# Softmax scaling on GpSimd and half the turned-probability copies on VectorE in the first block's attention

## What is computed

```python
def block_attention(q, k, v):            # q blocks of 128 rows
    s = jnp.einsum('bqhgd,bkhd->bhgqk', qi, k) * scale
    p = jax.nn.softmax(s, -1)
    return jnp.einsum('bhgqk,bkhd->bqhgd', p, v)
...
att_l = block_attention(q_l, [k_l; k_c], [v_l; v_c])
att_c = block_attention(q_c, k_c, v_c)   # layer 0 only
```

## Time and profile before

| what | us |
|---|---|
| median of three runs | 1950.0 |
| the three runs | 1945.93, 1950.0, 1954.12 |
| profiled execution, from its first to its last instruction | 1946.4 |
| attention of layer 0, from the first exponential to the last low part | 216.4 to 275.1 |
| attention of layer 1, the same | 849.5 to 887.3 |

### The profile page before, as it was taken

The page is one execution under the profiler, slowest core; times in us unless marked ns, Lnnn a source line. Parts: engine busy times, 40 slices in busy tenths (PEclk is TensorE's granted clock), DMA queues, the critical chain, the costliest instruction groups (busy, mean ns, idle before and its releaser), DMA issues.

```text
span 1946.4 us, 34448 instructions
## 1 busy us (share of the span) xinstructions
PE 1835.5 (94%) x15010; PEld 1624.3 (83%) x15010; DVE 1155.6 (59%) x1715; ACT 769.5 (40%) x1073; POOL 296.1 (15%) x264
## 2 busy tenths in 40 slices
PE   7999788999999988988999999989999999999998
PEld 5777556778888868857999999989988888899997
DVE  4644665654353347666665586555768778677654
ACT  4433563221122224355334443333455544344342
POOL 0011001999080010100000100003001111000000
PEclk9999999999999999899999999999999999999999
DMA  8245112666353222203555555544431112255551
GB/s 350 94 172 200 56 44 87 197 208 198 121 191 112 88 76 71 82 22 109 181 187 178 194 203 176 193 152 150 142 141 45 46 45 67 88 176 189 178 192 69
DMA packets 40759, 266.24 MB, mean 137 GB/s; under 512 B 4512, under 2 KB 4640, under 8 KB 13344
## 3 DMA queue, kind: packets, MB, share of 16 engines
q1 hardware_dynamic: 35712, 244.10, 36.2%
q0 software_dynamic: 4608, 16.78, 2.8%
q10 hardware_dynamic: 288, 3.15, 0.4%
HBM read 262.96 MB, written 1.05 MB: 136 GB/s over the span
## 4 chain that ended last, share of the span: by engine, by line
PE 77%; DVE 11%; ACT 5%; POOL 4%; issue 2%; DMA 1%; SPq 0%; DVEq 0%; ACTq 0%; POOLq 0%
PE ps L641 19%; PE ps L643 19%; PE ps L642 19%; DVE W L621 3%; PE ps L1666 2%; POOL work L1126 2%; DMA ring<-w_ada_dram 1%; PE ps L1028 1%; ACT W L612 1%; POOL work L1127 1%; PE ps L1453 1%; DVE work L821 1%; PE ps L2407 1%; PE ps L2425 1%; PE ps L647 1%
## 5 line engine op out<-in xcount | busy, mean ns | idle before, releaser
L621 DVE TENSOR_TENSOR W<-ring,W 128x2048 fp32r<-128x2048 f32 (+2 forms) x194 | 441.8, 2279 | 238.7 <-ACT W L612 238.4
L612 ACT ACTIVATE W<-ring 128x2048 fp32r<-128x2048 f32 (+2 forms) x194 | 359.0, 1853 | 114.0 <-PE ps L643 104.9
L641 PE MATMUL ps<-h_lat,W 128*128 128x256 f32 x1056 | 301.7, 286 | 5.9 <-DVE h_lat L813 4.0
L642 PE MATMUL ps<-h_lat,W 128*128 128x256 f32 x1056 | 300.6, 285 | 0.0
L643 PE MATMUL ps<-h_lat,W 128*128 128x256 f32 x1056 | 300.5, 285 | 0.0
L641 PEld LDWEIGHTS ps<-h_lat,W 128*128 128x128 f32 x1056 | 204.3, 193 | 7.1 <-issue 4.6
L642 PEld LDWEIGHTS ps<-h_lat,W 128*128 128x128 f32 x1056 | 204.2, 193 | 0.3 <-issue 0.2
L643 PEld LDWEIGHTS ps<-h_lat,W 128*128 128x128 f32 x1056 | 204.2, 193 | 0.0
L754 POOL TENSOR_TENSOR work<-work 128x256 f32<-128x256 f32 (+1 forms) x42 | 41.0, 976 | 951.8 <-ACT work L736 764.8
L1009 DVE TENSOR_TENSOR work<-work,ps 128x256 f32<-128x256 f32 (+1 forms) x88 | 43.0, 488 | 181.7 <-ACT work L984 181.6
L643 PE MATMUL ps<-hidden_lat,W 128*128 128x256 f32 x528 | 149.7, 284 | 0.0
(11 more groups left out here) (405 smaller groups left out, 4285.4 us busy)
## 6 DMA issues: line engine op xcount, KB each, us to landing
ring<-w_up_dram SPq DMA_DIRECT2D x88, 1024.0 KB, 4.9
ring<-w_down_dram SPq DMA_DIRECT2D x43, 1024.0 KB, 4.9
ring<-w_ada_dram SPq DMA_DIRECT2D x32, 1024.0 KB, 6.6
work<-w_ada_dram POOLq DMA_DIRECT2D x32, 512.0 KB, 4.2
ring<-w_rkv_dram SPq DMA_DIRECT2D x13, 1024.0 KB, 4.9
ring<-w_fm_dram SPq DMA_DIRECT2D x10, 1024.0 KB, 4.9
ring<-w_out_dram SPq DMA_DIRECT2D x8, 1024.0 KB, 4.9
ring<-w_gates_dram SPq DMA_DIRECT2D x16, 512.0 KB, 3.7
```

The lines of the kernel that those rows point to most:

```text
L612: act.activation(slots[SLOT[s]][:, 0, 0:cols], ring[:, u % RING, 0:cols], ACT.Copy).then_inc(w_high, 1)
L621: dve.tensor_tensor(slots[SLOT[s]][:, 1, 0:cols], ring[:, u % RING, 0:cols], slots[SLOT[s]][:, 0, 0:cols], ALU.subtract).then_inc(w_low, 1)
L641: pe.matmul(o, slots[SLOT[s]][:, 0, at:at + cols], high, start=first, stop=False)
L642: pe.matmul(o, slots[SLOT[s]][:, 0, at:at + cols], low, start=False, stop=False)
```

## The change

In both layers of the first block's attention, GpSimd multiplies the `probs` tile by the reciprocal of its sum in place of VectorE, in a loop over the units, `pool_attention`, that is put between `pool_mlstm` and `pool_sums`. VectorE keeps the reciprocal. The copy of the turned probabilities stays with ScalarE for even units and goes to VectorE for odd ones. VectorE issues the copy of unit i-3 in its step i (even i from 4 on), behind maximum and negative of unit i and ahead of the reciprocal of unit i-1. Three semaphores come in: `at_recip` (VectorE to GpSimd), `at_even` and `at_odd` (the copies). TensorE now waits for `at_even` and `at_odd` where it waited for `at_pt`, at the same places of its order. The second block's attention only counts `at_pt` from another start.

```diff
@@ pe_attention
-                    pe.wait_ge(at_pt, base + 2 * p + 2)
+                    pe.wait_ge(at_even, base // 2 + p + 1)
+                    pe.wait_ge(at_odd, base // 2 + p + 1)
...
-                            pe.wait_ge(at_pt, base + x - 1)
+                            pe.wait_ge(at_odd if x % 2 else at_even, base // 2 + x // 2)
@@ act_attention
-                if 2 <= i < n + 2:
+                if 2 <= i < n + 2 and i % 2 == 0:
                     x = i - 2
...
-                    act.activation(probsT[x % 4][:, 0:nk], ps[:, 6 + x % 2, 0:nk], ACT.Copy).then_inc(at_pt, 1)
+                    act.activation(probsT[x % 4][:, 0:nk], ps[:, 6, 0:nk], ACT.Copy).then_inc(at_even, 1)
@@ dve_attention
+                if 4 <= i < n + 4 and i % 2 == 0:
+                    x = i - 3
+                    nk = units[x][3]
+                    dve.wait_ge(at_t, base + x + 1)
+                    if x >= 4:
+                        dve.wait_ge(at_o, base + x - 3)
+                    dve.tensor_copy(probsT[x % 4][:, 0:nk], ps[:, 7, 0:nk]).then_inc(at_odd, 1)
                 if 1 <= i <= n:
                     x = i - 1
                     dve.wait_ge(at_exp, base + x + 1)
-                    link(dve.reciprocal(at_small[:, 3, x:x + 1], at_small[:, 2, x:x + 1]))
-                    pr = probs[x % 4][:, 0:units[x][3]]
-                    dve.tensor_scalar(pr, pr, at_small[:, 3, x:x + 1], None, ALU.mult).then_inc(at_p, 1)
+                    dve.reciprocal(at_small[:, 3, x:x + 1], at_small[:, 2, x:x + 1]).then_inc(at_recip, 1)
@@ new
+        def pool_attention(pool, layer):
+            units, base = attention_units(layer), AT_BASE[layer]
+            for x, (_, _, _, nk) in enumerate(units):
+                pool.wait_ge(at_recip, base + x + 1)
+                pr = probs[x % 4][:, 0:nk]
+                pool.tensor_scalar(pr, pr, at_small[:, 3, x:x + 1], None, ALU.mult).then_inc(at_p, 1)
```

More of the change, by code:

```diff
@@ L1411, in build @@
             sem(f"at_{x}") for x in ("scores", "max", "exp", "probs", "turned", "probsT", "o", "high", "out"))
+        at_recip, at_even, at_odd = (sem(f"at_{x}") for x in ("recip", "probsT_even", "probsT_odd"))
         def attention_units(layer):
@@ L2135, in pe_dilated @@
                 if x >= 1:
-                    pe.wait_ge(at_pt, SB + x)
+                    pe.wait_ge(at_pt, x)
                 for s in range(s_width(x) // P):
@@ L2143, in pe_dilated @@
                 b = 64 * (hh % 2)
-                pe.wait_ge(at_pt, SB + x + 1)
+                pe.wait_ge(at_pt, x + 1)
                 if x == 0:
@@ L3123, in _ @@
                 pool_mlstm(pool, layer)
+                pool_attention(pool, layer)
                 pool_sums(pool, 2 * layer + 1)
```

## The result

| kernel | median us | ratio to before | 95% interval |
|---|---|---|---|
| before | 1951.9 | 1 | |
| changed | 1981.5 | 1.0153 | 1.0129 to 1.0177 |

The account below looks back on a forecast made before the run. PV's wait for the odd copy, behind other work on its engine, was taken as the bound. Layer 0 (+5.1, +1.3, +2.6), layer 1 (+5.3), starts (+0.6) and clock (+1.0) gave 15.9, rounded to +16: 1966.0 us, range 1958 to 1979.

Parts of the forecast that it names:

- What bounds the kernel: Attention pairs: loop through TensorE and ScalarE, PV waiting for the copy behind the exponential; 3.78 us long, 2.49 short.
- The copy behind the maximum: VectorE's odd copy makes PV wait for later scores and maximum: 1.02 us more per long pair, 0.47 per short.
- the scaling on GpSimd: Scaling moved off VectorE: at most 1.29 and 0.74 us long, costing 0 to 0.05 us a pair, taken as 0.
- The slack of 1.40 and 0.75 us: Odd unit's turn: GpSimd's scaling may last 1.40 us in long and 0.75 in short pairs before it costs anything.
- a sign that it is wrong: Signs against the forecast: ScalarE releases PV, L1539 ends the turns' waits, or time between stages exceeds run-to-run difference.
- the clock: Behind the weight split, longer TensorE idling adds a slow loop per layer: 1.0 us for both layers, between 0 and 2.4.
- Start of a stage: PV of pair 0 waits for the copy in step 4: 0.3 us more in each layer.
- The split: Step 8's weight split ahead of unit 5's copy: two intervals take 13.7 us against 11.8, nothing added apart.
- A: Rival: faster, both copies ready when scores end, TensorE's own work bounds at 3.18 and 1.88 us; 1937.3 us, chance 0.04.
- B: Rival: no difference that counts, maximum gets its scores earlier and half the price goes; +8, 1958 us, chance 0.09.
- D: Rival: clock stays low throughout as TensorE's share falls to 66%; about 25 us more, 1991 us, chance 0.05.
- C: Rival: GpSimd becomes the bound, it and VectorE holding each other up at SBUF; some 14 us on top, 1980, chance 0.08.

Follow-up runs that it names:

- the run with filled waits: Changed kernel with transposes of the identity, whose results nobody reads, put into TensorE's waits: median 1971.3 us, ratio 1.0113.
- the run with the short scaling: Changed kernel with GpSimd's scaling written as a product of two tensors, the reciprocal repeated along the row: median 1975.7 us, ratio 1.0105.
- split moved: Kernel before with ScalarE's odd-step copy ahead of its exponential and step 8's weight split behind the attention's last step: 1940.3 us, ratio 0.9918.

## Why the prediction fell short, point by point

- **What bounds the kernel.** Right. PV waits for the odd copy, and the copy for what stands ahead of it on its engine. Moving ScalarE's copy alone made the kernel before faster.
- **The copy behind the maximum.** Right, term by term. 4.80 and 2.96 us were summed; with the scaling on VectorE the loops measure 4.84 and 3.01. The copy took 0.68 and 0.41 us, and PV waited behind the scores for 1.67 us in place of 1.62. Putting it ahead of the maximum gives 17.5 us back, of the 29.6. One reading beside it is off by a pair: TensorE turns pair k behind PV of pair k-1 and not before it, and the scores of pair k+2 come right behind those turns. The loop has the same steps either way.
- **The step that failed: the scaling on GpSimd.** The slack of 1.40 and 0.75 us was right to 0.06: passes of 0.96 and 1.08, 0.60 and 0.61 cost the loops nothing, 1.57 and 0.93 cost 0.23 and 0.24 us a pair. The bound was wrong. A pass with two tensor operands was taken as the upper end for one with a scalar from a column of SBUF, and the term was put at 0. This form took 1.57 us, 0.28 over that bound, and L1539 ended waits of the turns, which the prediction had named as a sign that it is wrong. By the two ways to take it out, this term is 8.6 or 9.4 us in the stages. Of the 9.4, 2.6 lie in the loops, 3.2 between the first maximum and the first PV, and 3.6 in the first interval behind it. There the turns wait for GpSimd itself (1.46 and 0.89 us ahead of the first two of layer 0), the clock then falls, and the run with filled waits shows 3.2 of those 3.6 us to be clock. Part of that is luck: in the changed kernel and the runs with the scaling alone and the copy ahead the clock fell at five of six stage starts, and at the sixth, with the same two waits (1.45 and 0.88 us), it held. The figure in the Trainium skill, 769 ns for 512 elements in the page "GPSIMD Engine Reference", section "Performance versus the Vector engine", is a best case there; this pass took twice that.
- **The step that was mis-sized: the clock.** 1.0 us was taken for both layers, 2.4 at most, on top of what the kernel before pays. That is 1.16 us in layer 0 (4.94 - 3.78) and about 0.99 in layer 1 (0.42 and 0.57), and it stands in the intervals to which the sum adds: 3.2 us in all. In the run with the short scaling the loop behind the split took 7.55 us in layer 0 and 7.03 in layer 1, where an undisturbed one takes 4.85: 2.7 + 2.2 = 4.9 us, 1.7 more than the sum holds. There was no further slow loop; the one slow loop in each layer cost more than twice as much. The price was taken from PV alone (1.98 in place of 1.09). In the new loop, PV, turns and scores all lie on the chain, and each of them takes longer.
- **Start of a stage.** Forecast at +0.3 us each. From the first maximum to the first PV the changed kernel takes 9.34 and 9.15 us against 6.89 and 6.36: +2.5 and +2.8. With the short scaling +0.8 and +1.2 are left, 1.4 us more than forecast. The other intervals of that run come out 1.1 us over the sum, in small pieces of 0.3 or less.
- **The split.** Right apart from the clock: with filled waits the two intervals around it take 8.91 + 5.07 = 14.0 us, against 13.7 forecast; in the changed kernel 8.91 + 7.29 = 16.2.
- **Rivals.** A and B are out, since the median moved by 29.6 us. D is out: at 66% of TensorE's time the clock held. In the last pairs of layer 0 the clock did fall in two of the runs with this loop, which cost 1 us. What A asked for, the copy ahead of the maximum, gave 3.67 us a long pair with the scaling on VectorE and 4.47 with it on GpSimd, not 3.18. C had the right time, 1980, and the right engine. Its mechanism was another one: negative and reciprocal lasted 0.21 and 0.15 us as before, 31 of GpSimd's 32 passes over 512 columns took 1.55 to 1.57 us, and only one was stretched to 1.83, beside VectorE's L1939; the form of the instruction set the length. The earlier trace rows give means of VectorE's side alone; that GpSimd's side grows as well stands in other rows of that trace, where its 128x1024 passes in L1126 take 1.92 or 3.01 us. That C's time fits is partly luck, since it was worked out for 2.0 and 1.1 us and without more of the low clock. The range stopped 1 us short of C's own figure.

Together: 15.9 forecast; 4.3 more with a scaling as short as assumed (1.7 behind the split by the clock, 1.4 at the starts, the rest in small pieces); and 9.4 for GpSimd's length with what it brings at the start, low clock included: 29.6.

## What to carry to other kernels

An engine's queue is a promise of order: before a copy is handed to a less busy engine, look at what will stand ahead of it there and what that waits for; here 17.5 us hung on one place in VectorE's queue, and 5 us on one in ScalarE's. A duration of another instruction form is no bound, even if that form reads more; the same product took 1.57 us in one form and 1.08 in the other. Where a new loop runs through TensorE from end to end, price a low clock on all of its steps.

## What the runs showed of the hardware

- GpSimd's product with a scalar from a column, 128 partitions in float32, took 1.57, 0.93 and 0.60 us at 512, 256 and 128 columns (0.96 as the mean of the run with half of the scaling, where single passes took up to 1.82), by estimate from these about 2.5 ns a column and 0.3 us more. The product with the same value repeated as a second tensor took 1.08 and 0.61 us at 512 and 256 (1.04 in 30 of the 32 long ones, 1.49 and 2.02 in the other two).
- The granted clock held at 1.00 with TensorE busy for 66% in short, even waits, and fell behind single waits of 3.9 and 5.6 us. At the start of the changed stage it fell with single waits of at most 1.8 us, and filling the waits kept it up. The same instructions do not always get the same clock: behind the wait of 1.75 us ahead of layer 0's second scores it fell in three of the twelve profiled executions (copies alone, scaling with two inputs, split moved) and held in nine. What exactly makes it fall was not taken apart.
